# Decode attention of a hybrid MLA/SSD/MoE step: every latent page requested by SyncE, only the rotary rows by GpSimd

## The reference, cut to what matters

```python
def mla_attend_sample(q_nope, q_pe, ckv, k_pe, cache_ckv, cache_kpe, layer, page_table, p):
    ckv_past = cache_ckv[layer, page_table].reshape(b, -1, KV_LORA)
    kpe_past = cache_kpe[layer, page_table].reshape(b, -1, QK_ROPE)
    q_lat = jnp.einsum('bshd,chd->bshc', q_nope, p['w_uk'])
    sc_past = jnp.einsum('bshc,btc->bhst', q_lat, ckv_past) + jnp.einsum('bshr,btr->bhst', q_pe, kpe_past)
...
    pr = jax.nn.softmax(sc, axis=-1).astype(ckv.dtype)
    o_lat = (jnp.einsum('bhst,btc->bshc', pr[..., :n_past], ckv_past)
             + jnp.einsum('bhst,btc->bshc', pr[..., n_past:], ckv))
```

## Time and profile before

| | us |
|---|---|
| median of 3 runs | 978.37 |
| the 3 runs | 978.37, 972.56, 978.42 |
| profiled execution, its own time | 973.75 |
| span of the profiled execution | 971.4 |
| decode attention, first transposes to last product (L933) | about 247 to 328 of the span |

### The profile page before, as it was taken

The page is one execution under the profiler, slowest core; times in us unless marked ns, Lnnn a source line. Parts: engine busy times, 40 slices in busy tenths (PEclk is TensorE's granted clock), DMA queues, the critical chain, the costliest instruction groups (busy, mean ns, idle before and its releaser), DMA issues.

```text
span 971.4 us, 18238 instructions
## 1 busy us (share of the span) xinstructions
PE 903.8 (93%) x7483; PEld 560.5 (58%) x7483; DVE 328.5 (34%) x822; ACT 197.1 (20%) x489; POOL 154.1 (16%) x185
## 2 busy tenths in 40 slices
PE   4799999997899699999889999999999999999996
PEld 3688888875556557756745445444445445445442
DVE  0423770046344597436222222221122222111124
ACT  2100110316122179033111111111111111111112
POOL 0000000032475000000122112121221211212110
PEclk9999999999999799999999999999999999999999
DMA  9886575626599457997799999999999999999962
GB/s 372 323 301 265 208 309 197 247 92 247 189 347 345 174 224 254 412 418 313 271 420 382 422 419 421 420 419 425 417 419 419 423 420 419 421 418 423 412 283 94
DMA packets 58917, 325.46 MB, mean 335 GB/s; under 512 B 16178, under 2 KB 25251, under 8 KB 37651
## 3 DMA queue, kind: packets, MB, share of 16 engines
q1 hardware_dynamic: 44930, 305.54, 77.8%
q0 software_dynamic: 12176, 18.56, 5.7%
q10 hardware_dynamic: 1728, 0.18, 0.1%
HBM read 326.65 MB, written 15.81 MB: 353 GB/s over the span
## 4 chain that ended last, share of the span: by engine, by line
PE 37%; DMA 13%; DVE 1%; issue 0%; ACT 0%; POOL 0%; POOLq 0%
PE bank L2235 18%; PE bank L2175 9%; DMA done_out<-in_w_e 7%; PE bank L2186 5%; DMA slot_b<-in_w_e 4%; PE bank L2153 3%; DMA xg<-tok_rows,tab_g 1%; PE bank L2221 1%; DMA weight_tab<-wgt 1%; PE bank L2267 1%; DVE slot_b L2560 0%; DVE slot_b L2568 0%; POOL weight_tab L2099 0%; PE bank L2205 0%; PE bank L2213 0%
## 5 line engine op out<-in xcount | busy, mean ns | idle before, releaser
L368 PE MATMUL bank<-h,ring 128*128 128x264 f32 x672 | 154.6, 391 | 2.4 <-DVE h L244 1.8
L368 PEld LDWEIGHTS bank<-h,ring 128*128 128x128 f32 x672 | 127.9, 192 | 26.6 <-issue 3.0
L2358 ACT ACTIVATE sge<-bank 64x256 f32<-64x256 f32 x64 | 24.1, 377 | 405.8 <-PE bank L2235 405.8
L2460 DVE TENSOR_TENSOR hh<-sge,bank 64x256 f32<-64x256 f32 x64 | 27.1, 423 | 230.5 <-ACT sge L2358 230.5
L2235 PE MATMUL bank<-done_out,xt 128*64 128x256 f32 x832 | 97.2, 387 | 2.9 <-DMA done_out<-in_w_e 2.9
L2235 PE MATMUL bank<-ring,xt 128*64 128x256 f32 x800 | 91.8, 382 | 2.2 <-DMA ring<-in_w_e 1.9
L1563 POOL DMA_INDIRECT xg<-tok_rows,tab_g x32 | 32.0, 999 | 336.6 <-PE bank L2153 324.1
L2401 DVE COPY sq<-bank 128x512 f32<-128x512 f32 x64 | 44.3, 692 | 102.1 <-PE bank L2175 102.0
L2235 PEld LDWEIGHTS bank<-done_out,xt 128*64 128x64 f32 x832 | 58.7, 138 | 31.6 <-DMA done_out<-in_w_e 3.3
L2175 PE MATMUL bank<-ring,ht 128*32 128x512 f32 x320 | 76.4, 598 | 0.0
L2186 PE MATMUL bank<-sq,wmat 64*128 64x512 f32 x256 | 71.9, 640 | 3.0 <-DVE wmat L2434 3.0
(11 more groups left out here) (478 smaller groups left out, 1213.8 us busy)
## 6 DMA issues: line engine op xcount, KB each, us to landing
ring<-in_w_units SPq DMA_DIRECT2D x28, 2048.0 KB, 10.7
done_out<-in_w_e SPq DMA_DIRECT2D x26, 2048.0 KB, 23.9
ring<-in_w_e SPq DMA_DIRECT2D x25, 2048.0 KB, 22.7
slot_b<-in_w_e SPq DMA_DIRECT2D x13, 2048.0 KB
ring<-in_w_e SPq DMA_DIRECT2D x20, 1024.0 KB, 24.0
slot_b<-in_w_e SPq DMA_DIRECT2D x11, 1024.0 KB, 26.7
done_out<-in_w_e SPq DMA_DIRECT2D x11, 1024.0 KB, 24.5
row_of<-in_w_e SPq DMA_DIRECT2D x11, 1024.0 KB, 26.6
```

Of the source, the lines that this page charges most:

```text
L368: mm = pe.matmul(bank[:, t % NB, 0:T], w[:, j, k, :], h[:, k, :], start=(k == 0), stop=(k == KD - 1))
L2358: act.activation(sg[e % 2][:, :], bank[0:LB, 4, 0:FE], ACT.Silu).then_inc(sg_ready, 1)
L2460: dve.tensor_tensor(hh[e % 2][:, :], sg[e % 2][:, :], bank[LB:2 * LB, 4, 0:FE], ALU.mult).then_inc(hh_ready, 1)
```

## The change

SyncE requests all four pages of each group, 16 a batch in place of 12, and reads 16 page numbers. GpSimd requests only the rotary rows, 4 a batch, and reads no page numbers. TensorE still waits for two semaphores for each group; their counts follow (64 increments from SP's transfers, 16 from POOL's). What is loaded, where to, which buffers there are and when they come free is as before.

```diff
-        fourth_in = [[sem(f"fourth_in{i}_{m}") for m in range(NPG // 4)] for i in range(3)]
+        rope_in = [[sem(f"rope_in{i}_{m}") for m in range(NPG // 4)] for i in range(3)]
...
-                def load_three(sp, b):
-                    rows = page_numbers(mybir.EngineType.SP, b, 0, 3)
+                def load_pages(sp, b):
+                    rows = page_numbers(mybir.EngineType.SP, b, 0, 4)
                     if b >= NBUF:
                         sp.wait_ge(weighed, b - NBUF + 1)
                     for m in range(GR):
-                        for g in range(3):
+                        for g in range(4):
                             load_page(sp, b, m, g, rows[g * GR + m], page_in)
 
-                def load_fourth(pool, b):
-                    rows = page_numbers(mybir.EngineType.Pool, b, 3, 4)
+                def load_ropes(pool, b):
                     if b >= NBUF:
                         pool.wait_ge(weighed, b - NBUF + 1)
                     for m in range(GR):
-                        load_page(pool, b, m, 3, rows[m], fourth_in)
                         pool.indirect_dma_start(rope[b % NBUF][:, m, :], None, io["cache_rope"],
...
-                                        pe.wait_ge(page_in[b % NBUF][m], 16 * 3 * (b // NBUF + 1))
-                                        pe.wait_ge(fourth_in[b % NBUF][m], 16 * 2 * (b // NBUF + 1))
+                                        pe.wait_ge(page_in[b % NBUF][m], 16 * 4 * (b // NBUF + 1))
+                                        pe.wait_ge(rope_in[b % NBUF][m], 16 * (b // NBUF + 1))
```

More of the change, by code:

```diff
@@ L567, in load_fourth @@
                     for m in range(GR):
-                        load_page(pool, b, m, 3, rows[m], fourth_in)
                         pool.indirect_dma_start(rope[b % NBUF][:, m, :], None, io["cache_rope"],
                                                 bass.IndirectOffsetOnAxis(ap=rope_at[:, b * GR + m:b * GR + m + 1].bitcast(U32), axis=0),
-                                                bounds_check=POOL * ROPE - 1, oob_is_err=False).then_inc(fourth_in[b % NBUF][m], 16)
+                                                bounds_check=POOL * ROPE - 1, oob_is_err=False).then_inc(rope_in[b % NBUF][m], 16)
                 own = ExitStack()
@@ L605, in _ @@
                             for b in range(NBUF - 1):
-                                load_fourth(pool, b)
+                                load_ropes(pool, b)
                         @block.sync
@@ L611, in _ @@
                             for b in range(NBUF - 1):
-                                load_three(sp, b)
+                                load_pages(sp, b)
                             store(sp, io["ckv"], ckv[:, :, :])
```

## The result

The changed kernel takes 990.59 us (median of 4 runs, 988.88 to 993.72), the kernel before 976.68 (4 runs, 972.56 to 978.42). The ratio is 1.014, with a 95% interval of 1.010 to 1.018, so it is slower by 14 us. The forecast was 976.6 with a range of 971 to 982. The profiled execution of the changed kernel took 993.72 us with a span of 991.8, against 973.75 and 971.4: these two executions are 20 us apart, 6 more than the medians.

What follows compares the result with a forecast made beforehand. It took TensorE as the attention's pace; SyncE's 9.75 us a batch would use up its 7.0 us of waiting and delay the last pages by 0.4, with TensorE's reaction +0.5 us: 976.6 us, range 971 to 982.

Steps and rivals of the forecast that it cites:

- What bounds the kernel now: Decode attention: TensorE sets the pace at 8.69 us a batch, loads close behind; better loading can give at most 3.9 us.
- the holes without a name: TensorE's first transposes in batches 3 and 5: three holes without a releaser, taken for GpSimd's fourth page or rotary rows.
- What the change takes off GpSimd: GpSimd's stream: a group costs about 1.34 us in place of 1.91, and the rotary rows are never last again.
- What it adds to SyncE: SyncE's queue: a batch of 16 requests costs 9.75 us, above TensorE's 8.69, so SyncE paces the loop from batch 3.
- the reading of page numbers: SyncE, each batch: four more page numbers at an estimated 0.055 us each, 0.22 us.
- the held-up requests: SyncE's page requests: some take 1.25 us in place of 0.33; none counted, though one in each of four batches adds 3.7.
- rival A: SyncE's queue is the bound and itself held up: slower, +4.2 us at 0.92 a batch, +10.5 at 2.5; chance 0.22.
- Rival B, faster landing: SyncE's pages land quicker without GpSimd's beside them: end at -1.5 us, -3.9 with all holes gone; chance 0.14.
- Rival C, the clock: More waiting brings TensorE's lower clock into the attention: 10 us at 0.68 cost about 3 us; 0.06 with anything elsewhere.
- SyncE still waits before batches 5 to 7: Sign in SyncE's queue in the attention that, if seen, makes the forecast wrong.
- the attention's end moves by more than 3 us: Sign at the end of the decode attention that, if seen, makes the forecast wrong.
- GpSimd's gathers are 1.34 us apart: Sign in GpSimd's stream listed as showing the forecast right.

Runs made afterwards that it cites:

- e17: Changed kernel without loading the fourth pages of batches 3 to 7, with eight semaphore counts and waits behind each GpSimd gather: 968.78 us, 0.995 times before.
- e9: Changed kernel with a direct request of 4 bytes by 128 on GpSimd behind each gather: 977.85 us, 1.004 times before.
- e10: Changed kernel with one semaphore count and a wait for it on GpSimd behind each gather, no work between: 977.65 us, 1.005 times before.
- e16: Changed kernel with eight semaphore counts and waits on GpSimd behind each gather: 978.64 us, 1.005 times before.
- e6: Changed kernel with one single-column memset behind each gather that nothing waits for: 993.32 us, 1.019 times before.
- e14: Changed kernel with one semaphore count on GpSimd behind each gather and no wait: 995.37 us, 1.020 times before.
- e18: Changed kernel with eight semaphore counts on GpSimd behind each gather and no waits: 993.92 us, 1.022 times before.
- e3: Changed kernel without the gathers of batches 3 to 7, which use the rotary rows of batches 0 to 2: 984.33 us, 1.011 times before.
- e2: Kernel before with only GpSimd's order altered, a batch's four gathers ahead of its four page requests: 993.81 us, 1.020 times before.
- e12: Kernel before with GpSimd's four gathers ahead of its four page requests, plus one count and wait behind each gather: 997.08 us, 1.021 times before.
- e15: Changed kernel without loading the fourth pages of batches 3 to 7, with one count and wait behind each gather: 992.81 us, 1.017 times before.
- e8: Changed kernel with only the fourth pages of groups 1 and 3 moved to SyncE and one chained memset between paired gathers: 976.91 us, 1.000 times before.
- e11: Changed kernel with only group 3's fourth page moved to SyncE and one chained memset a batch on GpSimd: 974.78 us, 1.000 times before.
- e13: Kernel before with GpSimd's four gathers ahead of its four page requests, plus a small chained memset behind each gather: 998.71 us, 1.023 times before.
- e7: Changed kernel with only the fourth pages of groups 1 and 3 moved to SyncE, so gathers come in pairs: 989.92 us, 1.013 times before.

## Why the prediction was wrong

**What bounds the kernel now: right.** TensorE was the pace, and 3.9 us was named as the most that better loading can give. e17 comes near it: with twelve requests on SyncE and free streams (the fourth pages of batches 3 to 7 are not loaded), its queue reads

```profile
286.61 6.47 SPq L552 DMA_DIRECT2D ring<-in_cache  x12
295.29 7.75 SPq L552 DMA_DIRECT2D page<-in_cache  x12
```

The last two batches begin 295.29 - 286.61 = 8.68 us apart, the 8.69 of a batch that waits for nothing, and ac goes out at 303.90, 3.6 us before its 307.52. The kernel is 4.7 us under before (3.0 to 6.4). That the holes without a name belong to GpSimd's transfers fits what follows, without being proved: in e9, e10, e16 and e17, whose streams are free and whose GpSimd requests no page, no transpose waits without a name, and in e10 all eight waits name a page, as the prediction said:

```profile
PE bank L854 <- DMA page<-in_cache: 3.5, 6, 1.5
PE bank L854 <- DMA ring<-in_cache: 2.7, 2, 1.6
```

**What the change takes off GpSimd: this step failed.** It said that a group would cost 1.34 us in place of 1.91, which is what happened (1.30), and that the rotary rows would never be last again; it counted no harm from it. (Its working is not consistent: 1.91 less 0.57 is 1.34, but less the 0.30 as well it is 1.04, and the 3.8 us for the memsets needs the latter. The rows show 1.00 and 0.30 for each gather, so the 0.30 stays.) The reason given was that GpSimd is busy 16% and short of time nowhere. That judged the engine by its own load. What it does to other engines' streams was no term of the sum, and no rival had it. The prediction counted each instruction that is moved, but asked only what it costs where it arrives and saves where it left. It did not ask what the moved request had kept apart: it was the separator of two gathers. The cost is the difference between the changed kernel and the same kernel with a separator, 0.010 of the time (1.014 against 1.004 in e9 and 1.005 in e10), some 10 us. In e6, e14 and e18, which differ from the changed kernel by next to nothing, it is 0.015 to 0.018.

**What it adds to SyncE: right in kind, up to 0.9 us a batch too small.** The kernels with free streams show it without the other effect, here e10:

```profile
261.31 9.17 SPq L552 DMA_DIRECT2D ring<-in_cache  x16
271.66 19.71 SPq L552 DMA_DIRECT2D page<-in_cache  x32
...
303.36 9.12 SPq L552 DMA_DIRECT2D page<-in_cache  x16
```

Batch 3 begins at 261.31, as predicted (261.58), and batch 7 at 303.36: 10.5 us a batch, where the sum had 9.75. (In e9 batch 7 begins at 300.94, 10.06 a batch, of which 1.0 us in all is waiting, so its queue alone needs 9.8; in e3 it is 10.3, in e16 10.7.) Of the terms, the reading of page numbers was right. It was estimated at 0.055 us for each more; it is 0.054:

```profile
L545 SPq TENSOR_LOAD <-ptab x8: 970/978/1178, 207.9 to 302.2; - x8
```

against 762 in the earlier trace rows, which makes the 0.22. The mis-sized term is the held-up requests, "I take none": the 16 of a batch take 9.1 to 9.6 us in e10 where 15 x 0.518 + 0.33 makes 8.10, some 1.0 to 1.5 more in each batch. The 0.518 was read off batch 3, the lightest of the loop. From the end of a batch's requests to the next batch it is 271.66 - 270.48 = 1.2 us, less than the 1.65 allowed, and that gives a part back. The transposes of group 3 of batch 7, which the sum put 0.44 us later than before, begin 1.8 us later in e9, 3.5 in e10 and 4.6 in e16. These kernels are 3.5 us (e9, 0.0036), 4.5 (e10) and 4.9 us (e16, 0.0050) slower. The mechanism is rival A, a queue that is the bound and is itself held up, near its first price of +4.2, and in e10 with its sign of batch 7 beginning after 303; the forecast's +0.5 was too small. Alone it would have stayed within 1%.

**Rival B, faster landing: half right and swallowed.** SyncE's pages from 246 to 330 us (count, KB, median us to landing), before and then changed:

```profile
page<-in_cache SPq DMA_DIRECT2D x38, 128.0 KB, 4.9
page<-in_cache SPq DMA_DIRECT2D x10, 256.0 KB, 7.9
```

```profile
page<-in_cache SPq DMA_DIRECT2D x38, 128.0 KB, 3.4
page<-in_cache SPq DMA_DIRECT2D x26, 256.0 KB, 3.8
```

That is 1.5 us quicker for the small pages and half the time for the large ones; in e10 the medians are 3.8 and 4.2. The rival's first sign, landings under 4 us, came true in the changed kernel; its second, fewer holes, did not: in e10 TensorE waits 6.2 us for pages where the holes before were 3.1, because the quicker transfers are requested later. The prediction said that no row shows the packets of the two queues apart. The pages of the profile do, in their third part: GpSimd's queue went from 12176 packets and 18.56 MB to 9616 and 10.17, SyncE's from 44930 and 305.54 MB to 49538 and 313.94. The moved pages were thus packets of 3.3 KB on GpSimd's queue and are packets of 1.8 KB on SyncE's. That fits the share that the rival gave SyncE's pages; that it is the cause of the quicker landing was not tested. The fit of 2.0 us plus bytes over 436 GB/s that the prediction put on SyncE's pages stands in the Trainium skill's "DMA: Bandwidth & Descriptors", section "Anatomy of one DMA — SWDGE (gpsimd) path", for the path of GpSimd's transfers only; where it made 2.6 us, the medians are 3.8 and 4.2.

**Rival C, the clock: the right fear, with a small price on it.** Three stages of the attention are at 0.83 where before had 1.00 in all from 250 to 320 us; a stage at 0.83 does 1.7 us less of full-clock work, the three together 5, which may be half of the 10. The price of "10 us at 0.68", about 3 us, was thus of the right size; only what brings it on was not foreseen. e3 shows it at its worst, 0.52 over 10 us. But the lower clock also comes where nothing is torn: e9 has 0.83 between 280 and 290 and is still only 0.4% slower. What share of the 10 us is the clock's and what the tearing's own was not measured apart.

**The signs that were named.** "SyncE still waits before batches 5 to 7" came true for batches 5 and 7 (not for 6), and "the attention's end moves by more than 3 us" with 16.1; both falsified the forecast. "GpSimd's gathers are 1.34 us apart" came true too, and was listed as a sign that all was well.

The Trainium skill's "DMA: Bandwidth & Descriptors", section "Issuing engines are not separate DMA queues", holds that requesting from several engines saves only the sequencer's time, usually small beside the transfer. The first cost contradicts this: at the 388 GB/s of the earlier trace rows a page of 128 KB is 0.34 us of transfer (an estimate), a request takes 0.52 to 0.6 us of SyncE, and SyncE's queue became the pace. The second cost, the larger one, is no sequencer time at all, and that section says nothing of it.

**What stays open.** That the gathers, following without a wait, hold up the other engines' streams is shown (e16 against e18, e10 against e14, before against e2). Why they do is not: no row names a releaser. Nor is it settled why one wait was enough in e10 and not in e12 and e15. A rival named before e16, that it depends on the chance position of the instructions, stays untested: every added wait moves them. It would hardly account for all seven kernels at 1.30 to 1.37 us without a wait being held up and all seven at 1.9 or more being free, but for the five with waits at 1.30 it could. A gather handed over while the last still runs would fit e14 and e18 but not those two. Whether 1.9 us with no separator at all would do was not tried; in the free kernels at that distance there is always a direct request or a chained memset between.

No version here beats the kernel before. e8 and e11, which move two and one of the four fourth pages and pace the gathers, equal it. e17 is faster, but loads fewer pages.

## What to carry to other kernels

When an instruction is taken off a lightly loaded engine, ask what it stood between, not only what it cost; in particular look at what its neighbours do once they touch. In a trace, an operand group torn in two with nothing to wait for, growing "issue" rows on several engines and "remote" rows appearing at the same moments point to something that holds up the instruction streams, and the engine whose activity coincides may be one that nobody waits for. Judge a test by the sign it is meant to show and not by its time alone: e13 was the slowest of all and had the fault removed.

## What the runs showed of the hardware that was not expected

- Indirect gathers of GpSimd (128 rows each, 1.0 us of its time) that follow one another at 1.30 us with no wait hold up TensorE, ScalarE, VectorE and SyncE: "issue" waits of up to 1.3 us at TensorE's rotary weight loads where 0.2 was the most, and 10 to 21 us of the kernel's time (changed kernel against e9, e18 against e16, e15 against e17). Two in a row are enough (e7). One burst of four was followed by a granted clock of 0.52 over 10 us (e3), the same burst in the changed kernel was not.
- A direct request of 128 x 4 bytes (0.59 us) or one chained memset (0.14 us, with 0.79 of idle time before the next gather) behind each gather removes it. Eight semaphore counts with waits remove it at an unchanged distance (e16, e17); eight counts without waits do not (e18), and one with a wait did in e10 and did not in e12 and e15.
- The time that a request takes of SyncE varies from batch to batch: before, 0.52 us apart in batch 3 and (8.50 - 0.33) / 11 = 0.74 in batch 7; in e10, where its queue is the pace, 0.59 in both ((9.17 - 0.33) / 15 in batch 3).
- A page of 256 KB requested by SyncE landed in 7.9 us (median) before, and in 3.8, 4.7 and 4.2 us in the changed kernel, e9 and e10. What of this is due to GpSimd's pages no longer running beside it was not separated.
